# Two transformer blocks on one core: operand buffers declared first, modulation products on TensorE, alternating bank sets, shifted chains, later low parts

## The reference

```python
mod = silu(c) @ w_ada + b_ada                  # 6 x 1024: shift1, scale1, gate1, shift2, scale2, gate2
h = rmsnorm(x, norm1_w) * (1 + scale1) + shift1
proj = h @ w_in                                # q, k, v, index q, k, w, retention q, k, v, gates
x = x + gate1 * (merged @ w_out)               # top-k attention and retention, gated, merged
h2 = rmsnorm(x, norm2_w) * (1 + scale2) + shift2
x = x + gate2 * ((silu(h2 @ w_ffn_gate) * (h2 @ w_ffn_up)) @ w_ffn_down)      # d_ff 2816
x = rmsnorm(x, final_norm_w)
# second block
z = rmsnorm(x, attn_norm) @ w_in_2             # keys, values, queries, linear-attention inputs, gates
x = x + concat(compressed + selected + window attention, gated linear attention) @ w_out_2
u = causal_conv3(rmsnorm(x, ffn_norm) @ w_up_2)
return x + (silu(gate(u)) * up(u)) @ w_down_2
```

## Time and profile before

| | |
|---|---|
| median of 3 runs | 1628.5 us |
| the profiled execution | 1628.07 us, span 1626.3 us, granted clock 0.994 |
| PE / PE weight load busy | 1590.8 us (98%) / 1268.0 us (78%) |
| DVE / ACT / POOL busy | 881.5 (54%) / 614.2 (38%) / 43.8 us (3%) |
| 128x512 products with wh, Hh / with wh, Hl / with wl, Hh | 408.8 / 392.6 / 392.2 us |
| chain that ended last | PE 91%, DVE 4%, ACT 2%, issue 1%, POOL 1% |
| DMA | 165.76 MB, mean 102 GB/s |

### The profile page before, as it was taken

One profiled execution on the slowest core, in us unless ns is written; L12 is line 12 of the kernel. 1 busy time (PEld: TensorE's weight loads), 2 busy tenths in 40 slices (PEclk: granted clock), 3 DMA queues, 4 the chain that ended last, 5 costly groups with the idle time before them and its releaser, 6 DMA issues.

```text
span 1626.3 us, 19784 instructions
## 1 busy us (share of the span) xinstructions
PE 1590.8 (98%) x8003; PEld 1268.0 (78%) x8003; DVE 881.5 (54%) x1628; ACT 614.2 (38%) x1069; POOL 43.8 (3%) x82
## 2 busy tenths in 40 slices
PE   6999999999999999999999999899999999999999
PEld 5877877678888888888888886666768888887887
DVE  6769785655375653232333655676457455555432
ACT  4443334542312432222322454466425334344320
POOL 1000000000000000000000101100000000000000
PEclk8999999999999999999999999999999999999999
DMA  7512121136245334322222151110113222222221
GB/s 299 198 65 103 53 75 69 53 129 246 104 168 168 104 131 155 104 91 101 86 99 99 34 188 47 39 53 14 40 53 116 91 104 91 88 85 100 104 78 52
DMA packets 44883, 165.76 MB, mean 102 GB/s; under 512 B 5108, under 2 KB 5236, under 8 KB 43640
## 3 DMA queue, kind: packets, MB, share of 16 engines
q1 hardware_dynamic: 44792, 164.50, 28.8%
HBM read 162.38 MB, written 2.10 MB: 101 GB/s over the span
## 4 chain that ended last, share of the span: by engine, by line
PE 91%; DVE 4%; ACT 2%; issue 1%; POOL 1%; DMA 0%; SPq 0%; DVEq 0%; ACTq 0%
PE bank L526 87%; PE bank L535 4%; DVE AR L1656 1%; DVE AR L1663 1%; DMA X<-in_x 0%; DVE wl L1644 0%; POOL ST L2420 0%; DVE X L1656 0%; ACT wh L1150 0%; ACT AR L1161 0%; ACT AR L1173 0%; DVE CST L1656 0%; POOL ST L2418 0%; DVE ST L1666 0%; DVE Hl L1656 0%
## 5 line engine op out<-in xcount | busy, mean ns | idle before, releaser
L526 PE MATMUL bank<-wh,Hh 128*128 128x512 f32 (+1 forms) x1008 | 408.8, 406 | 0.4 <-DVE wl L1644 0.4
L526 PE MATMUL bank<-wh,Hl 128*128 128x512 f32 (+1 forms) x1008 | 392.6, 390 | 0.0
L526 PE MATMUL bank<-wl,Hh 128*128 128x512 f32 (+1 forms) x1008 | 392.2, 389 | 0.0
L1150 ACT ACTIVATE wh<-raw 128x1024 fp32r<-128x1024 f32 (+2 forms) x195 | 203.6, 1047 | 403.6 <-PE bank L526 391.4
L1644 DVE TENSOR_TENSOR wl<-raw,wh 128x1024 fp32r<-128x1024 f32 (+2 forms) x195 | 234.3, 1209 | 138.9 <-ACT wh L1150 138.3
L526 PEld LDWEIGHTS bank<-wh,Hh 128*128 128x128 f32 x1008 | 190.5, 189 | 58.0 <-issue 21.7
L526 PEld LDWEIGHTS bank<-wh,Hl 128*128 128x128 f32 x1008 | 190.2, 189 | 40.5
L526 PEld LDWEIGHTS bank<-wl,Hh 128*128 128x128 f32 x1008 | 190.7, 189 | 34.3
L526 PE MATMUL bank<-Hh,wh 128*128 128x512 f32 (+2 forms) x504 | 190.5, 378 | 2.6 <-DVE AR L1663 1.2
L526 PE MATMUL bank<-Hh,wl 128*128 128x512 f32 (+2 forms) x504 | 189.4, 376 | 0.0
L526 PE MATMUL bank<-Hl,wh 128*128 128x512 f32 (+2 forms) x504 | 189.3, 376 | 0.0
(11 more groups left out here) (245 smaller groups left out, 1878.5 us busy)
## 6 DMA issues: line engine op xcount, KB each, us to landing
raw<-in_wst SPq DMA_DIRECT2D x268, 512.0 KB, 3.6
AR<-in_wst SPq DMA_DIRECT2D x8, 1024.0 KB, 6.5
X<-in_x SPq DMA_DIRECT2D x8, 512.0 KB, 4.9
AR<-in_wst SPq DMA_DIRECT2D x5, 512.0 KB, 6.0
out<-X SPq DMA_DIRECT2D x8, 256.0 KB, 2.1
CST<-in_cst SPq DMA_DIRECT2D x1, 1619.0 KB, 9.6
raw<-in_wst SPq DMA_DIRECT2D x4, 296.0 KB, 2.8
BC<-in_bc SPq DMA_DIRECT2D x2, 512.0 KB, 6.9
```

What stands on the lines that cost most here:

```text
L526: return e.matmul(o, l, r, start=start, stop=stop, skip_group_check=True)
L1150: e.activation(HI[slot[i]][:, 0:width(i)], raw[:, i % NR, 0:width(i)], ACT.Copy).then_inc(*w_hi.mark(i))
```

## The change

- Buffers: Hh, Hl, wh, wl, Ah/Al (with AF), EH/EL (with ACC) are declared first, then X, raw, AR, CST, PRMT, BC, G, MC, ST.
- Start: SP issues X0, parameters, constants, X1 to X3, modulation block 0, iq chunk 0, block 1, ik, block 2, and so on. `modulation_rows` puts the sum over a modulation block on PE: silu(c) stands in `SCZ`, one column of 32, the others zero; eight fp32 matmuls (32 stationary columns, 256 moving) go to the four 32-row strips of a bank in turn; VectorE copies the rows out, `modulation_columns` adds over the partitions with two one-column matmuls. For blocks 4, 6 and 7 (`ADDED`) VectorE makes the row in eight operations spread over steps. The first block's rows are put between the transposes of tiles 2 and 3. The last tile's rows are copied out by ScalarE alone; the first two feature chunks are made by VectorE beside ScalarE's high part.
- Banks: up block j has banks 0 to 3 if j is even, 4 to 7 if odd; the first chunk of a down stage goes through tiles 2, 3, 0, 1. The decays use banks 4, 5 and 3, 6 in turn; the compressed keys' second layer goes to bank 7 instead of 6.
- Chains: decays start after 1 step instead of 3, with more steps between Ln and the products; queries of tiles 2 and 3 are scaled 10 steps after, turned 13 and 14 steps after their tile; in `linear`, VectorE's scaling comes one step after its sum.
- Low parts: outside iq, a low part comes two steps after its high part.

The diff; left out are the renaming of banks at places that only follow the two sets, and unchanged lines:

```diff
@@ -268,7 +268,8 @@
-    lows, used, load = [], set(range(NP)), NP + NR
+    later, lows, used, load = [], [], set(range(NP)), NP + NR
@@ -276,9 +277,10 @@
-        done[k] += lows
-        used |= set(lows)
-        lows = []
+        due = later if name != "iq" else later + lows
+        later, lows = (lows, []) if name != "iq" else ([], [])
+        done[k] += due
+        used |= set(due)
@@ -327,27 +329,28 @@
         def sem(name):
...
-        X = sb("X", [P, T, D])
...
-        raw = sb("raw", [P, NR, 1024])
...
+        with nc.sbuf_tensor("Ah", [P, 4, S], f32r) as Ah, nc.sbuf_tensor("Al", [P, 4, S], f32r) as Al:
+            pass
+        AF = sb("AF", [P, 8, S])
+        with nc.sbuf_tensor("EH", [P, 2, S], f32r) as EH, nc.sbuf_tensor("EL", [P, 2, S], f32r) as EL:
+            pass
+        ACC = sb("ACC", [P, 2, D])
+        X = sb("X", [P, T, D])
+        raw = sb("raw", [P, NR, 1024])
...
-        with nc.sbuf_tensor("EH", [P, 2, S], f32r) as EH, nc.sbuf_tensor("EL", [P, 2, S], f32r) as EL:
-            pass
-        ACC = sb("ACC", [P, 2, D])
...
-        with nc.sbuf_tensor("Ah", [P, 4, S], f32r) as Ah, nc.sbuf_tensor("Al", [P, 4, S], f32r) as Al:
-            pass
-        AF = sb("AF", [P, 8, S])
@@ -405,7 +408,9 @@
-        PART = [[G[:, 512 * i + 256 * j:512 * i + 256 * j + 256] for j in (0, 1)] for i in (0, 1)]
+        SCZ = ST[:, 64:320].rearrange("p (q c) -> p q c", q=8)
+        MROW = [G[:, 256 * i:256 * i + 256] for i in (0, 1)]
@@ -416,6 +421,15 @@
         def norm_banks(tag, t):
...
+        ADDED = (4, 6, 7)
+        def mod_bank(k):
+            return 5 + k % 3 if k else 0
+        def up_bank(j, m):
+            return m + 4 * (j % 2)
@@ -493,6 +507,7 @@
+        DECAY = ((4, 5), (3, 6))
@@ -613,28 +628,35 @@
-                    free[b] = (act.of((tag, "gained", t)), dve.of((tag, "gained", t)))[n]
-            on.wait_ge(s_cst, 16)
-            for t in range(T):
-                norm_turn("n1", t)
-            def modulation(k):
-                b, part, land = 6 + k % 2, PART[k % 2], LAND[k % 4]
-                on.wait_ge(*act.of(("silu c",)))
-                on.wait_ge(*dve.of(("sum", k)))
+                    free[b] = act.of((tag, "gained", t)) if n == 0 or (tag, t) == ("n1", 3) else dve.of((tag, "gained", t))
+            def modulation_rows(k):
+                b = mod_bank(k)
+                on.wait_ge(*dve.of(("spread",)))
+                on.wait_ge(s_pre[k % 4], 16 * (k // 4 + 1))
...
+                for q in range(8):
+                    r = slice(32 * (q % 4), 32 * (q % 4) + 32)
+                    x = mm(bank[b][r, 0:256], SCZ[:, q, :], LAND[k % 4][:, q, :], q < 4, q >= 4)
+                x.then_inc(*small.mark(("mod rows", k)))
+            def modulation_columns(k):
+                b = mod_bank(k)
+                on.wait_ge(*dve.of(("mod rows", k)))
...
-                    o = bank[b][:, m:m + 1]
-                    mm(o, part[0][:, tok(m)], C("ones", 0, 1), True, False)
-                    mm(o, part[1][:, tok(m)], C("ones", 0, 1), False, False)
-                    x = mm(o, land[:, 7, tok(m)], SC[:, 7:8], False, True)
+                    x = mm(bank[b][:, 256 + m:257 + m], MROW[k % 2][:, tok(m)], C("ones", 0, 1), True, True)
...
-            modulation(0)
-            modulation(1)
+            on.wait_ge(s_cst, 16)
+            for t in range(3):
+                norm_turn("n1", t)
+            modulation_rows(0)
+            norm_turn("n1", 3)
+            modulation_columns(0)
+            modulation_rows(1)
@@ -661,7 +683,11 @@
-                        modulation(k + 2)
+                        modulation_columns(k + 2)
+                if (k, t) == (0, 0):
+                    modulation_columns(1)
+                if t == 2 and k + 2 < 8 and k + 2 not in ADDED:
+                    modulation_rows(k + 2)
@@ -856,19 +882,20 @@
+                        b = up_bank(j, m)
...
-                            claim(m)
+                            claim(b)
...
-                            x = mm3(bank[m][:, a:a + n], (h[:, q, tok(m)], l[:, q, tok(m)]), (Hh[:, k, a:a + n], Hl[:, k, a:a + n]), k == 0, k == 7)
+                            x = mm3(bank[b][:, a:a + n], (h[:, q, tok(m)], l[:, q, tok(m)]), (Hh[:, k, a:a + n], Hl[:, k, a:a + n]), k == 0, k == 7)
...
-                            free[m] = freed(j, m)
+                            free[b] = freed(j, m)
             def down(key, freed, each=lambda t: None):
@@ -882,10 +909,12 @@
-                    for tt in range(T) if t is None else (t,):
+                    tiles = ((2, 3, 0, 1) if k == 0 else range(T)) if t is None else (t,)
+                    for tt in tiles:
...
-                            events = [(key, t, n)] * (k == 21) + [("used", place[key, k])] * (n == 1 and tt == T - 1)
+                            events = [(key, t, n)] * (k == 21) + [("used", place[key, k])] * (n == 1 and tt == (1 if k == 0 else T - 1))
@@ -1006,8 +1035,7 @@
             def decays():
-                for _ in range(3):
-                    yield
+                yield
@@ -1015,26 +1043,26 @@
-                for _ in range(3):
+                for _ in range(5):
...
                 for t in range(T):
...
-                    l = T2[t][:, 256:512]
+                    l, (b0, b1) = T2[t][:, 256:512], DECAY[t % 2]
...
-                    claim(4)
-                    mm(bank[4][:, 0:256], C("upto"), l, True, True).then_inc(*small.mark(("upto", t)))
-                    free[4] = act.of(("e2", t))
-                    claim(5)
-                    mm(bank[5][:, 0:256], C("after"), l, True, True).then_inc(*small.mark(("after", t)))
-                    free[5] = act.of(("kd", t))
+                    claim(b0)
+                    mm(bank[b0][:, 0:256], C("upto"), l, True, True).then_inc(*small.mark(("upto", t)))
+                    free[b0] = act.of(("e2", t))
+                    claim(b1)
+                    mm(bank[b1][:, 0:256], C("after"), l, True, True).then_inc(*small.mark(("after", t)))
+                    free[b1] = act.of(("kd", t))
                     for j in range(2):
-                        x = mm(bank[5][:, 256 + 2 * j:258 + 2 * j], l[:, tok(j)], C("half"), True, True)
+                        x = mm(bank[b1][:, 256 + 2 * j:258 + 2 * j], l[:, tok(j)], C("half"), True, True)
...
-                    lambda t: w.after(7, lambda: turn_heads("nq", t, 2, TN[t], dve.of(("nq", "roped", t)))), 2)
+                    lambda t: w.after((7, 7, 13, 14)[t], lambda: turn_heads("nq", t, 2, TN[t], dve.of(("nq", "roped", t)))), 2)
@@ -1190,27 +1218,31 @@
             def rows_out(t):
...
-                e.activation(AF[:, 0:4, tok(t)], bank[norm_banks("n1", t)[0]][:, :].rearrange("p (j q) -> p j q", j=4), ACT.Copy).then_inc(
-                    *act.mark(("n1", "gained", t)))
+                x = e.activation(AF[:, 0:4, tok(t)], bank[norm_banks("n1", t)[0]][:, :].rearrange("p (j q) -> p j q", j=4), ACT.Copy)
+                if t == T - 1:
+                    x.then_inc(*act.mark())
+                    on.wait_ge(*small.of(("n1", "turned", t, 1)))
+                    x = e.activation(AF[:, 4:8, tok(t)], bank[norm_banks("n1", t)[1]][:, :].rearrange("p (j q) -> p j q", j=4), ACT.Copy)
+                x.then_inc(*act.mark(("n1", "gained", t)))
...
             def features(k):
...
-                on.wait_ge(*dve.of(("n1", "gained", T - 1)))
+                on.wait_ge(*dve.of(("n1", "gained", T - 2)))
...
-                e.activation(FUL[k % 2], AF[:, k, :], ACT.Identity, scale=gain, bias=shift).then_inc(*act.mark())
+                    e.activation(FUL[k % 2], AF[:, k, :], ACT.Identity, scale=gain, bias=shift).then_inc(*act.mark())
...
-                if t:
-                    rows_out(t - 1)
-            rows_out(T - 1)
+            for t in range(T):
+                if t == 3:
+                    split_high(place["iq", 0])
+                rows_out(t)
...
-            split_high(place["iq", 0])
@@ -1462,7 +1494,7 @@
-                w.after(15 if name == "ks" else 10, lambda: [out_(u) for u in (0, 1)])
+                w.after(15 if name == "ks" else 11, lambda: [out_(u) for u in (0, 1)])
@@ -1522,16 +1553,18 @@
+                for _ in range(4):
+                    yield
...
-                yield
                 for t in range(T):
...
+                    b0, b1 = DECAY[t % 2]
@@ -1541,7 +1574,7 @@
-                    w.after(7, lambda t=t: heads_out("nq", t, 2, qT))
+                    w.after((7, 7, 13, 14)[t], lambda t=t: heads_out("nq", t, 2, qT))
@@ -1701,24 +1739,43 @@
-            def modulate(k):
-                land, part = LAND[k % 4], PART[k % 2]
-                on.wait_ge(*act.of(("silu c",)))
+            def modulation_rows(k):
+                on.wait_ge(*small.of(("mod rows", k)))
+                if k >= 2:
+                    on.wait_ge(*small.of(("modulation", k - 2)))
+                copy(MROW[k % 2], bank[mod_bank(k)][:, 0:256], ("mod rows", k))
```

(87 more changed lines are left out.)

26 lines of the change are left out of this document (12 added, 14 removed).

## The result

The changed kernel takes **1611.6 us** (median of 4 runs, 1606.8 to 1612.8) against 1628.9: ratio 0.989, 95% interval 0.9865 to 0.9916. The forecast was 1607, range 1597 to 1618, faster at 0.90. The profiled execution is the fastest of the four: its span went from 1626.3 to 1605.0, 21.3 us, where the medians differ by 17.3.

What follows compares the result with a forecast made beforehand. TensorE, busy 98% of the span, was taken to bound the kernel; gains of 6.0, 5.5, 2.1, 3.0, 5.0 and 0 sum to 21.6 us, taken from 1628.07 to forecast 1607 us, range 1597 to 1618.

Steps and rivals of the forecast that it cites:

- Part 1: Buffer places: 1200 512-column products with Ah or Al go from 232 to 227 ns, start to start; 6.0 us gained.
- Rival (a): Buffer place is not the cause of the 5 ns; Ah and Al products keep 232 ns, 1612.5 us; chance 0.13.
- Part 2: Kernel start: X loads before modulation weights, row sums on PE; first dense product at 20.5 against 25.98, 5.5 us gained.
- rival (b): The modulation row blocks on PE do not overlap, 3.4 us each warm; 1618 us; chance 0.08.
- Part 3: Stage iq: cheaper modulation blocks and less low clock take it from 37.0 to 34.9 us; 2.1 us gained.
- Part 4: Up and down stages: two bank sets and down's tile order remove PE's waits for banks; 3.0 us gained, bounds 2 to 3.6.
- the four waits: PE's waits for banks: 0.37 in the first up stage, 0.66 and 0.59 in the second, 1.26 at the second down.
- part 6: Low parts two steps behind, outside iq: stalls gained and lost balance; 0, bounds 1.5 gained and 4 lost.
- Part 5: Linear part and second attention, 985 to 1036 us: chains moved a step apart; 5.0 us gained, bounds -1 to 9.
- the waits for the maximum and kc: PE's 1.5 and 1.8 us behind DVE's query scalings at the second attention; later scaling removes them, up to 2.2 coming back.
- The Gelu wait: PE's 3.1 us wait for ScalarE's Gelu in the linear part; earlier decays take 1.8 off, leaving near 1.2.
- rival (d): Low parts come too late in short steps: 60 chunks each stall PE 0.45 us, 27 us lost, 1633.5; chance 0.05.

Runs made afterwards that it cites:

- two shifts: 128 bytes declared ahead of Ah in the kernel before, 1618.4 us; 384 bytes ahead of Ah in the changed kernel, 1623.3 us; one run each.
- the second execution: The changed kernel run and profiled once more, unaltered: median 1616.1 us, its profiled run 1617.4 us.

## Why the prediction was right, and where it was not

The direction and the time were within the forecast. Step by step, against the profiled execution:

- **Part 1** (6.0 us, measured 7.0): the 1200 products and the 5 ns were read rightly from the starts, and the groups went to 389 to 390 as said. The cause was named wrong. "What is slow begins above 186 KB" fell with two shifts; the clause behind it, "or goes with Ah's address in some other way", was the right one, though it spoke of Ah's own start, and it is the difference from the other operand's. Rival (a) is out. The Trainium skill, "TensorE: Matmul & The Clock Gate", section "Back-to-back issue gap", gives its 216 ns for a product by itself, and for a stream of weight loads and 512-column products about 131 ns. No group in any run shows a sign of either: the best is 226 to 227 ns. And the Trainium skill, "SBUF — State Buffer", section "Operand start alignment", says of its rule that it is about legality, not speed; here starts that are legal differ by 5 ns a product.
- **Part 2** (5.5, measured 6.75): X3's square came at 9.89, against 9.6 to 10.2. The first row block took 1.14 us with a part at the low clock, a block at the full clock 1.00, where 2.1 and 1.15 had been forecast: that 1.14 looks like 1.15 is luck. The four column groups do run side by side, 0.21 us for four records, so rival (b) is out. By the Trainium skill's "TensorEngine Tiling (Array Packing)", section "Key Properties", a change of mode drains TensorE; 1.00 us against the 0.85 of four quarters side by side leaves room for 0.15 at the edges, and no run shows what of it is the drain. Off by size: I let the clock be low for all of the start, and it was full from 14.1 us on in this execution (that the transposes before stand at the low clock, 213 ns apart, was right, though the windows read 1.00 there). What is late now is not "PE's own queue" but the second block of weights, ik's (the chain has 11.26 us of DMA up to 16.88), ScalarE's high part of it, and the first features; taking the features first gave 0.6.
- **Part 3** (2.1, measured 1.95): iq lasts 35.1 us, 35 was forecast, but by errors that cancel. The row blocks took 1.00 us instead of 1.15 and the 1 us booked for the low clock was not lost, while two waits of 0.5 and 0.4 us that the forecast did not have came at 39 and 48. In the second execution, with the low clock from 19.4 on, iq lasts 36.7 us.
- **Part 4** (3.0, measured 3.9, above its bound of 3.6): the four waits went, and 0.25 us with each instead of 0.05. Missed: that the second set also covers waits which part 6 makes.
- **Part 5** (5.0; 8.0 in the first trace, 3.7 by medians): the waits for the maximum and kc went, and came back by about 0.9 rather than 2.2. The Gelu wait did not fall to 1.2: ScalarE is done in time, and DVE's copy of its result, behind 2.1 us of waiting for POOL and 2.2 us of scaling, is late in its place (2.5). The later scaling in `linear`, "on PE 0.2", gave 1.1; the wait of 1.5 us stands in every kernel without that edit and in none with it, but no run has it undone by itself, so the cause is argued and not shown. The forecast looked at the engine that ended the wait, and not at who comes next.
- **Part 6** (0, bounds 1.5 gained and 4 lost; measured -5.7 in waits, -11.7 by medians) is the step that failed. "The low parts come too late in the short steps" was rival (d), 27 us at 0.05, and it is not what happened either: the short steps pass without a wait. The forecast counted DVE's lead and never asked what else the low part does: it frees the raw buffer, and so starts the next load, and it stands in DVE's queue ahead of what PE needs next. The fall from 138.3 to 44.3 us that I took as relief gave PE nothing: with one step the 135.2 us are back and the kernel is faster.

The number 1607 was near because part 6's loss, over its bound of 4, was paid by what the other parts gave above their estimates, in the profiled execution at least. That these cancel is luck. The median of all nine runs of the changed kernel is 1613.0, 6 above the forecast.

## To carry to other kernels

Before an instruction is moved later, list what it releases, down to the transfer that waits for the buffer, and what will then stand behind it in its engine's queue; a long wait of an engine with time to spare may be the lead of a prefetch. Give the two operands of back-to-back 512-column fp32r matmuls starts that agree modulo 256 bytes (only multiples of 128 bytes were tried). When the profiled execution and the median differ, compare the granted clocks first, and where the clock's record has not begun, the distance of the starts.

## What the runs showed of the hardware

- A 128x512 product of fp32r parts whose moving and stationary operand start at places that differ by 128 bytes modulo 256 takes 232 to 233 ns from start to start, one whose starts agree modulo 256 takes 226 to 227; seen for (0,128), (128,0) and (0,384) against (128,128), (128,384) and (0,0), as remainders modulo 512.
- Sixteen records of fp32 products with 32 stationary columns in four column groups, 256 columns each, take 1.00 us at the full clock from their start to that of what follows, 0.21 for four side by side.
- PE's first transposes stand 213 ns apart and from about 14.1 us on 109 to 110, though the granted clock of the windows reads 1.00 throughout: the clock's record begins at that change.
- Which waits are followed by the 1.2 GHz level differs between executions of one kernel: the wait at 502 to 508 was followed by it in one execution of the changed kernel and not in another, and the medians carry it.
